# Two-layer conditioned trunk on one core: where the quads that come back from memory are split into high and low parts

## What is computed

```
def swiglu(h, w1, w3, w2):
    return (jax.nn.silu(h @ w1) * (h @ w3)) @ w2

shift, scale, gate = jnp.split(c_act @ ada_w[layer, 1] + ada_b[layer, 1], 3, axis=-1)
hn = rmsnorm(x, norm_g[layer, 1]) * (1.0 + scale[:, None, :]) + shift[:, None, :]
x = x + gate[:, None, :] * swiglu(hn, ffn_w1[layer], ffn_w3[layer], ffn_w2[layer])
```

## Time and profile before

| | |
|---|---|
| device time, median of 3 runs | 2290.47 us (2287.95 to 2292.0) |
| the profiled execution | 2293.13 us |
| its span, first to last instruction | 2291.4 us |
| granted TensorE clock, mean | 0.998 |
| PE busy | 2267.3 us (99%) |
| DVE busy | 1633.8 us (71%) |
| ACT busy | 965.6 us (42%) |
| queue q1 (SP's loads and stores), share of 16 DMA engines | 75% |

### The profile page before, as it was taken

One profiled execution on the slowest core, in us unless ns is written; L12 is line 12 of the kernel. 1 busy time (PEld: TensorE's weight loads), 2 busy tenths in 40 slices (PEclk: granted clock), 3 DMA queues, 4 the chain that ended last, 5 costly groups with the idle time before them and its releaser, 6 DMA issues.

```text
span 2291.4 us, 28351 instructions
## 1 busy us (share of the span) xinstructions
PE 2267.3 (99%) x10930; PEld 1893.9 (83%) x10930; DVE 1633.8 (71%) x1833; ACT 965.6 (42%) x1152; POOL 153.5 (7%) x145
## 2 busy tenths in 40 slices
PE   9999999999999999999999999999999999999998
PEld 6678888888888888888888888888888888888886
DVE  6777889876787677767987766798666645555557
ACT  2021443544334443344455555545444344434443
POOL 0000006100000000000510000250000000000000
PEclk9999999999999999999999999999999999999999
DMA  9999888678877997789877666576797566655674
GB/s 391 421 421 421 322 328 296 238 276 299 289 282 290 297 317 285 288 290 315 316 287 272 258 248 254 223 274 255 278 307 278 185 210 214 217 185 201 203 231 172
DMA packets 148473, 637.79 MB, mean 278 GB/s; under 512 B 69633, under 2 KB 69893, under 8 KB 73097
## 3 DMA queue, kind: packets, MB, share of 16 engines
q1 hardware_dynamic: 146754, 631.43, 75.0%
q10 hardware_dynamic: 1608, 4.84, 0.6%
HBM read 626.77 MB, written 9.46 MB: 278 GB/s over the span
## 4 chain that ended last, share of the span: by engine, by line
PE 61%; DMA 1%; DVE 1%; SPq 0%; issue 0%; ACT 0%; ACTq 0%; DVEq 0%
PE ps L1589 39%; PE ps L1691 13%; PE ps L1689 3%; PE ps L1694 3%; PE ps L1542 1%; DMA adaw<-ada_dram 1%; PE ps L1525 0%; PE ps L1833 0%; DVE wlow L1006 0%; PE ps L1859 0%; PE ps L1844 0%; PE ps L1567 0%; SPq L562 0%; SPq L580 0%; PE ps L1527 0%
## 5 line engine op out<-in xcount | busy, mean ns | idle before, releaser
L1006 DVE TENSOR_TENSOR wlow<-raw,whigh 128x1024 fp32r<-128x1024 f32 (+1 forms) x688 | 834.1, 1222 | 441.0 <-ACT whigh L712 433.1
L712 ACT ACTIVATE whigh<-raw 128x1024 fp32r<-128x1024 f32 (+1 forms) x688 | 716.4, 1045 | 882.2 <-PE ps L1589 584.1
L1589 PE MATMUL ps<-whigh,hn 128*128 128x512 f32 x2816 | 870.4, 389 | 0.0
L1589 PEld LDWEIGHTS ps<-whigh,hn 128*128 128x128 f32 x2816 | 528.6, 188 | 109.1
L1589 PE MATMUL ps<-wlow,hn 128*128 128x512 f32 x1408 | 547.8, 389 | 0.0
L1014 DVE CUSTOM_DVE_ANT_0 adaw<-adaw,cact 128x2048 f32<-128x2048 f32 x152 | 354.2, 2331 | 37.6 <-DMA adaw<-ada_dram 36.9
L1691 PE MATMUL ps<-mid,whigh 128*128 128x512 f32 x1152 | 366.0, 398 | 0.5 <-issue 0.3
L1589 PEld LDWEIGHTS ps<-wlow,hn 128*128 128x128 f32 x1408 | 264.3, 188 | 54.9
L1691 PE MATMUL ps<-hn,whigh 128*128 128x512 f32 x672 | 214.0, 397 | 0.0
L1589 PE MATMUL ps<-whigh,mid 128*128 128x512 f32 x680 | 210.8, 389 | 0.0
L1691 PEld LDWEIGHTS ps<-mid,whigh 128*128 128x128 f32 x1152 | 177.4, 190 | 1.7 <-issue 1.4
(11 more groups left out here) (247 smaller groups left out, 1657.7 us busy)
## 6 DMA issues: line engine op xcount, KB each, us to landing
raw<-wts_dram SPq DMA_DIRECT2D x386, 1024.0 KB, 4.9
adaw<-ada_dram SPq DMA_DIRECT2D x152, 1024.0 KB, 7.3
adaw_more<-ada_dram SPq DMA_DIRECT2D x24, 1024.0 KB, 15.5
raw<-ada_dram SPq DMA_DIRECT2D x16, 1024.0 KB, 12.5
hidden_dram<-work SPq DMA_DIRECT2D x56, 128.0 KB, 5.9
work<-hidden_dram SPq DMA_DIRECT2D x56, 128.0 KB, 7.0
work<-wts_dram SPq DMA_DIRECT2D x6, 1024.0 KB, 13.7
x<-xT_dram SPq DMA_DIRECT2D x4, 512.0 KB, 5.4
```

The lines of the kernel that those rows point to most:

```text
L712: act.activation(split_place((2 * s + h) % 4, width, spare)[0], raw[:, place, h * HALF:h * HALF + width], ACT.Copy)\
L1006: dve.tensor_tensor(low, raw[:, place_of(s, skips), h * HALF:h * HALF + width], high.bitcast(F32), ALU.subtract)\
L1589: ins = pe.matmul(ps[:, bank_, :], src[:, kk, a, tok], b[:, w], start=first, stop=kk == final and a == 1, skip_group_check=True)
```

## The change

The high part of a quad that comes back from memory is taken by ACT at step 3 of the `values` body, behind the first split of that step, and no longer at the start of step 2. The low part is taken by DVE at step 3 too, behind the product and before the second split of that step. As the earlier quads' lows are now made later, `turn_quad` no longer asks for those of its own group, but only for those of the groups before.

```diff
@@ scalar, body @@
-                    if kind[:6] == "values" and i and s == 2:
-                        tile, count = turned_quad(kind, q, i)
-                        act.wait_ge(S["blocks_landed"], 64 * quads_sent(kind, q, i))
-                        act.activation(mid[:, tile:tile + QUAD, 0, :], hidden_landing, ACT.Copy).then_inc(S["hidden_high"], QUAD)
...
                     if ahead:
                         split(*chunk, 0, spare=spare)
+                    if kind[:6] == "values" and i and s == 3:
+                        tile, count = turned_quad(kind, q, i)
+                        act.wait_ge(S["blocks_landed"], 64 * quads_sent(kind, q, i))
+                        act.activation(mid[:, tile:tile + QUAD, 0, :], hidden_landing, ACT.Copy).then_inc(S["hidden_high"], QUAD)
@@ vector, body @@
-                    if kind[:6] == "values" and i and s == 2:
-                        tile, count = turned_quad(kind, q, i)
-                        dve.wait_ge(S["hidden_high"], count + QUAD)
-                        m = mid[:, tile:tile + QUAD, :, :]
-                        dve.tensor_tensor(m[:, :, 1, :], hidden_landing, m[:, :, 0, :].bitcast(F32), ALU.subtract).then_inc(S["hidden_ready"], QUAD)
...
                         dve.wait_ge(S["hidden_product"], count + QUAD)
                         dve.wait_ge(S["chunks_evicted"], n * CH + CREDIT)
                         dve.sem_inc(S["chunks_evicted"], CH)
+                        if i:
+                            tile, count = turned_quad(kind, q, i)
+                            dve.wait_ge(S["hidden_high"], count + QUAD)
+                            m = mid[:, tile:tile + QUAD, :, :]
+                            dve.tensor_tensor(m[:, :, 1, :], hidden_landing, m[:, :, 0, :].bitcast(F32), ALU.subtract).then_inc(S["hidden_ready"], QUAD)
@@ tensor, turn_quad @@
                 pe.wait_ge(S["hidden_product"], count + QUAD)
-                pe.wait_ge(S["hidden_ready"], count)
+                pe.wait_ge(S["hidden_ready"], quad(kind, q, 0)[1])
```

## The result

| | before | changed |
|---|---|---|
| device time, median of 20 runs each | 2288.23 us (2284.37 to 2294.82) | 2293.31 us (2288.47 to 2302.57) |
| ratio changed / before | | 1.0024, 95% interval 1.0015 to 1.0034 |
| the profiled execution | 2293.13 us | 2291.81 us |

The changed kernel is slower by 0.24%, 5.5 us (3.4 to 7.8). The two profiled executions stand the other way round. That is no contradiction: both kernels scatter by 10 to 14 us from run to run, and the profile before was taken from one of the longer ones. What scatters is shown further down.

The account below looks back on a forecast made before the run. PE was taken as the bound, busy 2267.3 of 2291.4 us, so only its gaps counted. Direct waits of 1.7 plus later landings of 4.7 gave 6.4 us over 2290.5, so 2296.9; range 2289.5 to 2300.

Parts of the forecast that it names:

- R2: Rival: the product comes in time, so the long PE gaps and slow clock go; 8.0 us faster, 2282.5; chance 0.12.
- B: First down body of layer 0, group 1, at 873; PE gap before 2.73 us; late landing forecast to add 2.0.
- (1): PE waits directly for the moved low behind the transposes in the down body; 1.7 us in sum.
- A: First down body of layer 0, group 0, at 604; PE gap before 2.66 us; late landing forecast to add 1.0.
- C: First down body of layer 0, group 2, at 1094; PE gap before 0.29 us; late landing forecast to add 1.0.
- (2): SP's request behind the product goes out 1.14 us later, so the next unit 1 lands later; 4.7 us in sum.
- R1: Rival: the queue makes up the late request, leaving only the direct waits; +1.7 us, 2292.2; chance 0.23.
- R3: Rival: the clock falls at C as at A; a further +1.7 us, 2298.6; chance 0.10.
- (b): Sign: PE's gap before the transposes is 3 to 4 us at A, 4 to 5 at B, over 1 at C.
- D: First down body of layer 1, group 0, at 1738; no PE gap before; late landing forecast to add 0.7.
- (c): Sign: a new PE gap of about 0.5 us behind the transposes at B and C, ended by the moved low.
- (d): Sign: earlier values bodies' request comes 4.0 us after product start, not 2.7; next pair's unit 1 lands 1 us later.

Follow-up runs that it names:

- e1: Kernel before, with the quad taken late only in the last values body of each group, at step 2 in earlier ones; 1.0012, +2.7 us.
- e2: Kernel before, with the quad taken late only in the earlier values bodies, at step 2 in the last of each group; 1.0021, +4.8 us.
- e4: Changed kernel, with the low of the earlier values bodies moved behind the second split and block turn; 1.0021, +4.8 us against before.
- e12: Changed kernel, with the earlier values bodies' low moved into the next gates body, behind both splits of its step 0; 1.0011, +2.5 us against before.
- e3: Changed kernel plus one more DVE operation ahead of the second split in the earlier values bodies; 1.0060, +13.7 us against before.
- e7: Changed kernel plus one more DVE operation at the start of step 2 of the earlier values bodies; 1.0027, +6.2 us against before.
- e8: Kernel before plus one more DVE operation behind the product, ahead of the second split, in the earlier values bodies; 1.0025, +5.7 us.
- e10: Changed kernel, with DVE's unit 1 moved behind product, second split and block turn in the earlier values bodies only; 1.0005 against before.
- e5: Kernel before, with DVE's unit 1 of every values body moved to the end of step 3; 1.0014, +3.2 us.
- e6: Changed kernel, with DVE's unit 1 of every values body moved to the end of step 3; 1.0036, +8.2 us against before.

## Why the prediction was right, step by step

- **Who holds the product** (unit 1's landing, not the quad): right. The freed DVE stands 4.51 us for the unit, and R2, a gain by taking the quad out of the way, is refuted. The reading rested on B alone, where DVE waited for the load in the profile before; at the other places its last low ended within 0.1 us of the landing, and a reader who looked only at those would have been free to think either.
- **(1), PE's direct waits, 1.7 us:** mechanism and places right, the size too small. In e1, from start to start, PE loses 0.8 us at A (forecast 0.1), 1.1 at B (0.5) and 1.1 at C (1.1), 3.0 together; timed, e1 is +2.7 us (0.7 to 4.8). The step that was off: the forecast took the turned quad's lows at A and B as in time, because it reckoned with the slow clock there. With the clock at 1.00, as in e1, PE comes to them sooner and waits a second time. In the changed kernel's own profile (1) shows with 1.1 at C and, counted the same way, with 0.2 at A, where the product is in time; B is at the slow clock.
- **(2), the shift of the landings, 4.7 us:** the size was right: e2 is +4.8 us (2.7 to 7.1). The share that passes was set at 1.0 of 1.14; the growth of the lateness is 0.95 - (-0.12) = 1.1 (0.3 to 1.9) with requests late by 1.2. The step that was incomplete within it is the route. I named the request for the chunk of step 1 alone; the trace shows the second request late by as much. e4 frees the first alone and is still +4.8, e12 frees both and is at +2.5; as their intervals overlap, the weight of each isn't shown. The rows of the chain had shown the second.
- **(3), the relaxed wait of `turn_quad`,** taken as 0: no run keeps the old wait together with the late low, so neither the 0 nor the 1.4 us in three places was tested.
- **The sum**, 6.4 us over the median: measured 5.5 (3.4 to 7.8) by the ratio. The base was off, by no step of the change: 2290.5 was the median of 3 runs, 20 give 2288.2, so that the measured 2293.3 lies under the forecast of 2296.9 by 3.6 us though the difference is off by only 0.9. That it came so near is in part luck. (1) was worth 2.7 to 3.0 us where it was timed and traced alone, not 1.7, and e1 and e2 add up to 7.5, 2 more than the whole (within the intervals). The range of 2289.5 to 2300 was twice as wide as the effect and held R1, R3 and R4 too, so that the time alone says little; the mechanism rests on e2, e3, e7, e8 and e10.
- **What the profile would show:** (a), ACT's idle time gone, is right. (b) mostly missed: the gap grew at B, but to 3.33 us where 4 to 5 was forecast; at A (forecast 3 to 4) and at C before the transposes (over 1) there is none; at D it is 1.31, for which (2) had 0.7. The step behind this is that I took the lateness with which a group begins as fixed, from one execution. It is not: see below. (c) is right at C (0.39); at B it is hidden in the stretch at the slow clock, and e1 shows it with 0.48. (d) is right: 3.92 us for 4.0, and the lateness grows by 1.15 us a pair on the mean of five (0.06 before). The 0.6 us of stall in a `gates` body that (2) saw at B isn't in this profile.
- **R1** (the queue makes it up) is refuted by e2, e3 and e8, **R4** by the timing. **R3**, the clock at C, is not seen in the changed kernel's profile, where C has two short gaps and 1.00; it is seen in e3 with a gap of 4.79 us, and in e5 with one of 2.12 us (granted clock 0.66 over 1090 to 1095). The length of the gap alone doesn't decide: behind 2.59 us at A in e2 and 2.67 us at C in e6 the granted clock is 1.00 (over 604 to 608 and 1097 to 1101).
- **Left open:** how the loss divides between the two requests, why the landing of a fetched quad scatters, and what decides whether the clock falls behind a gap of 2 to 3 us.

## What to carry to other kernels

An engine's long wait is worth nothing if another wait ends at the same moment behind it: look for the one execution or place where the two part, before moving work. When an engine's work is followed by requests for loads, and these loads gate the same work one round later, its place relative to the requests counts more than its place relative to the consumer; 1.2 us put ahead of a request cost in every round here, and the same 1.2 us put where the engine stands anyway cost nothing that could be measured here. And a single profile of a kernel that scatters by 10 us shows one draw: take its gaps off its own time and see whether what is left agrees with a second profile, before adding differences to a median.

## What was not expected

The fetch of group 0's first quad through memory takes from 7.5 to 12 us, by its last part, though the kernels don't differ ahead of it. The issue and the landing of group 0's first fetch, in the kernel before, its second profile, and the changed kernel:

```profile
L589 SPq DMA_DIRECT2D work<-hidden_dram x4: 353/419/421, 537.3 to 538.6; - x4
...
DMA to landing us min/median/max: 7.3/8.0/12.0
```

```profile
L589 SPq DMA_DIRECT2D work<-hidden_dram x4: 354/419/422, 537.3 to 538.6; - x4
...
DMA to landing us min/median/max: 7.6/8.2/10.6
```

```profile
L589 SPq DMA_DIRECT2D work<-hidden_dram x4: 353/419/422, 537.5 to 538.8; - x4
...
DMA to landing us min/median/max: 6.2/6.4/7.5
```

The loads behind it in the queue land later by as much, so that unit 1 lands 13.4 us after its issue in the first and 8.8 us (550.96 - 542.16) in the last. The product of that body then starts at 558.70 in the first and at 555.32, with the body's end, in the last. So a group begins with its product in time or over 3 us late, and on the mean the loop makes up next to nothing (-0.12 us per pair).

But this start is only a part of the scatter. From one pair to the next the lateness moves by -2.2 to 2.8 us even where the requests are on time. Between the two profiles of the kernel before, the units of this first pair land 1.4 us apart, measured against their bodies, and those of the next, at A, 4.2 us apart: A has a gap of 2.66 us in one and none in the other. By the account above the gaps and falls are all of the 7.5 us between these two executions; that they are most of the scatter in the others, which have no profile, is likely and not shown.
